# Indexer dots of two pieces in four banks, linear-attention outputs two chunks at a time, and a compression with operands swapped on column halves

## The reference, cut to what matters

```python
# front, NSA: 31 overlapping blocks of 32 tokens, 2 groups, keys and values
blk = kv[:, idx] + pe[None, None, :, None, :]
hid = silu(einsum('bnlgd,ldh->bngh', blk, w1))      # contraction over 32*64 = 2048, 128 hidden
kc_or_vc = einsum('bngh,hd->bngd', hid, w2)
nsa_gates = sigmoid(h @ w_in[:, 1792:1816])          # 24 columns
# layers, indexer: 8 heads of 64, for each block of 128 queries
dots = einsum('bqhd,bsd->bqhs', iqb, ik) * IDX_HD ** -0.5
score = einsum('bqhs,bqh->bqs', relu(dots), iwb)     # then the top 128 keys of each query
# layers, linear attention: 8 chunks of 64 tokens, 4 heads, keys of 64, values of 128
S_c = a * S_{c-1} + u_c
o = einsum('bnchk,nbhkv->bnchv', q, states)          # chunk c reads S_c
```

## Time and profile before

| | |
|---|---|
| median of 3 runs | 1949.58 us (1949.49 to 1950.72) |
| the profiled execution | 1950.57 us, its span 1948.8 us |
| PE busy | 1929.9 us (99%), 9837 matmul records |
| ACT, DVE, POOL busy | 894.7, 1159.9, 342.5 us (46%, 60%, 18%) |
| granted TensorE clock | 1.0 of full speed over the span |
| DMA | 178.87 MB, mean 92 GB/s |

### The profile page before, as it was taken

The page is one execution under the profiler, slowest core; times in us unless marked ns, Lnnn a source line. Parts: engine busy times, 40 slices in busy tenths (PEclk is TensorE's granted clock), DMA queues, the critical chain, the costliest instruction groups (busy, mean ns, idle before and its releaser), DMA issues.

```text
span 1948.8 us, 25508 instructions
## 1 busy us (share of the span) xinstructions
PE 1929.9 (99%) x9837; PEld 1559.7 (80%) x9837; DVE 1159.9 (60%) x1862; ACT 894.7 (46%) x1427; POOL 342.5 (18%) x172
## 2 busy tenths in 40 slices
PE   9999999999999999999999999999999999999999
PEld 7977777888888887788887787888788888788787
DVE  6867546585453557687555545466589545555443
ACT  5544455543333345533445454445443444545432
POOL 1010002211120122254010010232235110010211
PEclk9999999999999999999999999999999999999999
DMA  6211103223222333223122123224222212122321
GB/s 232 93 65 44 65 23 141 97 86 108 87 107 86 108 112 128 85 87 108 44 92 82 46 87 130 87 86 151 87 87 87 87 47 105 44 90 87 117 100 65
DMA packets 25735, 178.87 MB, mean 92 GB/s; under 512 B 2976, under 2 KB 3616, under 8 KB 5408
## 3 DMA queue, kind: packets, MB, share of 16 engines
q1 hardware_dynamic: 23904, 164.24, 23.4%
q10 hardware_dynamic: 1728, 13.24, 1.8%
HBM read 171.18 MB, written 6.29 MB: 91 GB/s over the span
## 4 chain that ended last, share of the span: by engine, by line
PE 94%; ACT 2%; DVE 2%; POOL 1%; DMA 1%; issue 0%; DVEq 0%; SPq 0%; ACTq 0%; POOLq 0%
PE pp L278 31%; PE pp L282 15%; PE pp L268 10%; PE pp L270 10%; PE pp L269 10%; PE po L278 3%; PE po L282 2%; PE po L805 1%; PE ps L1147 1%; PE ps L724 1%; PE pt L775 1%; PE ps L1098 1%; PE po L1082 1%; PE po L1034 1%; PE pt L1068 1%; DMA wraw<-weights 1%
## 5 line engine op out<-in xcount | busy, mean ns | idle before, releaser
L262 DVE TENSOR_TENSOR wlo<-wraw,whi 128x2048 fp32r<-128x2048 f32 x124 | 291.8, 2353 | 254.2 <-ACT whi L257 253.6
L257 ACT ACTIVATE whi<-wraw 128x2048 fp32r<-128x2048 f32 x150 | 286.3, 1909 | 48.5 <-PE pp L282 48.4
L278 PE MATMUL pp<-hhi,whi 128*128 128x512 f32 (+1 forms) x704 | 287.0, 408 | 1.0 <-DVE hlo L473 0.8
L278 PE MATMUL pp<-hlo,whi 128*128 128x512 f32 (+1 forms) x704 | 275.3, 391 | 0.0
L278 PE MATMUL pp<-whi,hhi 128*128 128x512 f32 x464 | 192.2, 414 | 0.0
L282 PE MATMUL pp<-hhi,wlo 128*128 128x512 f32 (+1 forms) x704 | 190.1, 390 | 0.0
L278 PE MATMUL pp<-whi,hlo 128*128 128x512 f32 x464 | 181.6, 391 | 0.0
L268 PE MATMUL pp<-split,whi 128*128 128x512 f32 x420 | 163.8, 390 | 0.0
L270 PE MATMUL pp<-split,wlo 128*128 128x512 f32 x420 | 163.4, 389 | 0.0
L269 PE MATMUL pp<-split,whi 128*128 128x512 f32 x420 | 163.4, 389 | 0.0
L1860 POOL TENSOR_TENSOR wlo<-wraw,whi 128x2048 fp32r<-128x2048 f32 x26 | 120.5, 4633 | 220.0 <-ACT whi L257 220.0
(11 more groups left out here) (419 smaller groups left out, 3476.9 us busy)
## 6 DMA issues: line engine op xcount, KB each, us to landing
wraw<-weights SPq DMA_DIRECT2D x150, 1024.0 KB, 4.8
out_t<-xT ACTq DMA_DIRECT2D x4, 1024.0 KB, 3.9
xT<-out_t ACTq DMA_DIRECT2D x2, 2048.0 KB, 8.7
wraw<-weights SPq DMA_DIRECT2D x4, 512.0 KB, 8.3
xT<-x_t SPq DMA_DIRECT2D x4, 512.0 KB, 8.8
work<-cmp_w ACTq DMA_DIRECT2D x1, 2048.0 KB, 7.5
xT<-x_t ACTq DMA_DIRECT2D x1, 2048.0 KB, 7.9
out_t<-xT SPq DMA_DIRECT2D x4, 512.0 KB, 2.6
```

Source lines behind the costliest of these rows:

```text
L257: nc.scalar.activation(whi[:, slot, :], wraw[:, slot, :], ACT.Copy).then_inc(w_hi, 1)
L262: nc.vector.tensor_tensor(wlo[:, slot, :], wraw[:, slot, :], whi[:, slot, :].bitcast(F32), ALU.subtract).then_inc(w_lo, 1)
L278: nc.tensor.matmul(out_ap, *pair, start=(start and n == 0 and part == 0), stop=False)
```

## The change

Four things, in the order of the diff: the indexer's dots of pieces p-1 and p are issued one behind the other after the `pe_wide` of the odd piece p, even pieces in `ps` and odd ones in `pt`; the turn of the head weights moves to p = 0 and to columns 480 to 511 of `pt[0]`, with a new wait `iw_kept` before the dots of piece 1. The outputs of chunks c-2 and c-1 are issued together at even c, ahead of `u`. The front's compression has the blocks stationary (62 columns) and w1 moving (128), keys on output partitions 0 to 61 and values on 64 to 125, alternating; its result is turned by two transposes between the tiles of `ksw`. The 24 gate columns are stored twice in the weight chunk, the second copy is overwritten by the low part (DVE works on 24 columns of each step in place of a whole chunk), and a step is one matmul with 48 and one with 24 stationary columns; the two sets of 24 rows are added where they are turned, by a float32 matmul with two stacked identities, and Sigmoid comes after it.

```diff
+        def dot_bank(p, g):
+            return (ps, pt)[p % 2][g]
         def pe_dots(pe, l, p):
...
-            if e >= 2:
-                pe.wait_ge(ix_relu, e)
+            if e >= 4:
+                pe.wait_ge(ix_relu, e - 2)
             for x, y in ((0, 0), (0, 1), (1, 0)):
                 for g in range(2):
-                    last = nc.tensor.matmul(ps[g][:, 0:w], iqr[x][rows, hp, i * P:i * P + P], ikr[y][rows, 0:w],
+                    last = nc.tensor.matmul(dot_bank(p, g)[:, 0:w], iqr[x][rows, hp, i * P:i * P + P], ikr[y][rows, 0:w],
...
@@ pe_layer, for p in range(12)
-                if p == 1:
+                if p == 0:
                     pe.wait_ge(evac, section("ikg", l)[2] + 1)
                     for i in range(QT):
-                        last = nc.tensor.matmul(pt[0][:, 8 * i:8 * i + 8], alr_f[64:72, i * P:i * P + P],
+                        last = nc.tensor.matmul(pt[0][:, 480 + 8 * i:488 + 8 * i], alr_f[64:72, i * P:i * P + P],
                                                 ident[64:72, 64:72], start=True, stop=True)
                     last.then_inc(iw_turned, 1)
-                pe_dots(pe, l, p)
+                if p % 2 == 1:
+                    pe_dots(pe, l, p - 1)
+                    if p == 1:
+                        pe.wait_ge(iw_kept, l + 1)
+                    pe_dots(pe, l, p)
...
@@ pe_layer, for c in range(8 + 1)
+                for past in (c - 2, c - 1) if c >= 2 and c % 2 == 0 else ():
+                    i = past // 2
+                    pe.wait_ge(state_ready, 8 * l + past + 1)
+                    if past >= 2:
+                        pe.wait_ge(go_out, 8 * l + past - 1)
+                    for hd in range(4):
...
+                    last.then_inc(gla_o, 1)
                 if c < 8:
...
-                        if c >= 2:
-                            pe.wait_ge(state_ready, 8 * l + c)
...
                     pe_wide(pe, "gz", l, c)
-                if c >= 1:
-                    i = (c - 1) // 2
...
@@ act_layer: the copies of outputs c-2 and c-1 at even c, and behind them act_wide of gz
...
@@ front, PE
+            pe.wait_ge(blk_ready, 2)
+            for x in range(16):
+                for kv in range(2):
+                    last = nc.tensor.matmul(ps[kv][hid_rows(kv), 0:P], blk_f[kv][:, x, :], w1_f[:, 16 * kv + x, :],
+                                            start=(x == 0), stop=(x == 15))
...
+            pe_tm_tile(pe, "ksw", None, 0)
+            pe_tm_tile(pe, "ksw", None, 1)
+            pe.wait_ge(hid_silu, 2)
             for kv in range(2):
-                pe.wait_ge(blk_ready, kv + 1)
-                for x in range(16):
-                    last = nc.tensor.matmul(ps[kv][:, 0:2 * N_CMP], w1_f[:, 16 * kv + x, :], blk_f[kv][:, x, :],
-                                            start=(x == 0), stop=(x == 15))
-                last.then_inc(hid_done, 1)
-            pe_tm(pe, "ksw", None, 256)
-            pe.wait_ge(hid_out, 1)
+                nc.tensor.transpose(pt[kv][:, 0:2 * N_CMP], hid_s[hid_rows(kv), :],
+                                    ident[hid_rows(kv), hid_rows(kv)]).then_inc(hid_turned, 1)
+            pe_tm_tile(pe, "ksw", None, 2)
+            pe_tm_tile(pe, "ksw", None, 3)
+            pe.wait_ge(hid_out, 2)
...
             def gates(bank):
                 for x in range(KT):
-                    last = three(bank[0:24, :], (wh[:, x, 0:24], wl[:, x, 0:24]), (hhi[:, x, :], hlo[:, x, :]),
-                                 x == 0, x == KT - 1)
-                return last
+                    if x < KT - 1:
+                        nc.tensor.matmul(bank[0:48, :], wh[:, x, 0:48], hhi[:, x, :], start=(x == 0), stop=False)
+                    last = nc.tensor.matmul(bank[0:24, :], wh[:, x, 0:24], hlo[:, x, :], start=False, stop=False)
+                return nc.tensor.matmul(bank[0:48, :], wh[:, KT - 1, 0:48], hhi[:, KT - 1, :], start=False, stop=True)
...
             for i in range(QT):
-                last = nc.tensor.transpose(po[0][:, 24 * i:24 * i + 24], g_fm[0:24, i * P:i * P + P],
-                                           ident[0:24, 0:24])
+                last = nc.tensor.matmul(po[0][:, 24 * i:24 * i + 24], g_fm[0:48, i * P:i * P + P],
+                                        cst[0:48, C_TWO:C_TWO + 24], start=True, stop=True)
@@ front, ACT: Silu on token rows, copies of the turned result after tile 1 of ksw
+            for kv in range(2):
+                act.wait_ge(hid_done, kv + 1)
+                nc.scalar.activation(hid_s[hid_rows(kv), :], ps[kv][hid_rows(kv), 0:P], ACT.Silu).then_inc(hid_silu, 1)
...
+            for n in range(QT):
+                act_tm_tile(act, "ksw", None, n, k_tm[:, n, :])
+                if n == 1:
+                    act.wait_ge(hid_turned, 1)
+                    nc.scalar.activation(hid_f[:, 0:2 * N_CMP], pt[0][:, 0:2 * N_CMP], ACT.Copy).then_inc(hid_out, 1)
...
@@ front, DVE, in place of dve_next(dve, "ksw", None)
+            nc.vector.tensor_tensor(low, wraw[:, slot, :].rearrange("p (k n) -> p k n", k=KT)[:, :, 24:48], low.bitcast(F32),
+                                    ALU.subtract).then_inc(w_lo, 1)
```

More of the change, by code:

```diff
@@ L72 @@
 C_E128 = 467
-NCST = 482
+C_TWO = 482
+NCST = 506
 M_ID, M_TRI, M_CH, M_CMP = 0, 128, 256, 384
@@ L604, in two_block_kernel @@
         blk_f = [wv(T + 4096 + 992 * kv, 16, 2 * N_CMP) for kv in range(2)]
-        hid_f = [wv(T + 6080 + 64 * kv, 64) for kv in range(2)]
+        hid_f, hid_s = wv(T + 6080, 64), wv(15168, P)
         cw2 = wv(T + 6208, 2, P)
@@ L1350, in pe_layer @@
             for c in range(8 + 1):
+                for past in (c - 2, c - 1) if c >= 2 and c % 2 == 0 else ():
[4 more added lines that the diff above has]
+                    for hd in range(4):
+                        rows, at = y_rows(hd % 2), P * (hd // 2)
+                        bank = D_BANKS[2 * (past % 2) + hd % 2]
+                        last = nc.tensor.matmul(bank[:, at:at + P], gq_f[rows, hd // 2, P * i:P * i + P],
+                                                st_f[past % 2][rows, hd // 2, :],
+                                                start=True, stop=True)
+                    last.then_inc(gla_o, 1)
                 if c < 8:
@@ L1559, in act_layer @@
                     act.dma_start(xT[:, :, :], out).then_inc(x_back, 16)
-                if c >= 1:
-                    i, rows = (c - 1) // 2, y_rows((c - 1) % 2)
-                    act.wait_ge(gla_o, 8 * l + c)
+                for past in (c - 2, c - 1) if c >= 2 and c % 2 == 0 else ():
+                    i, rows = past // 2, y_rows(past % 2)
+                    act.wait_ge(gla_o, 8 * l + past + 1)
                     for g in range(2):
-                        bank = D_BANKS[2 * ((c - 1) % 2) + g]
+                        bank = D_BANKS[2 * (past % 2) + g]
                         dst = a_f[rows, i, :].rearrange("p (h g d) -> p h g d", h=2, g=2)[:, :, g, :]
@@ L1567, in act_layer @@
                     last.then_inc(go_out, 1)
+                if half == 1:
+                    act_wide(act, "gz", l, t, z_a[:, t, :], ACT.Silu)
                 if c == 5:
@@ L2127, in _ @@
                                  bias=con(C_EPS)).then_inc(tm_root, 1)
-            act_tiles(act, "ksw", None, lambda bank, n, m: nc.scalar.activation(k_tm[:, m, :], bank[:, 0:256], ACT.Copy))
+            for n in range(QT):
[3 more added lines that the diff above has]
+                    nc.scalar.activation(hid_f[:, 0:2 * N_CMP], pt[0][:, 0:2 * N_CMP], ACT.Copy).then_inc(hid_out, 1)
+                    act.wait_ge(hid_turned, 2)
+                    for g in range(2):
+                        last = nc.scalar.activation(hidr[:, g, :, 0:N_CMP], pt[1][:, N_CMP * g:N_CMP * g + N_CMP].unsqueeze(1)
+                                                    .broadcast_to([P, 4, N_CMP]), ACT.Copy)
+                    last.then_inc(hid_out, 1)
             act.wait_ge(kvc_done, 1)
@@ L2459, in _ @@
             dve.drain().then_inc(tm_fin, 1)
-            dve_next(dve, "ksw", None)
+            c0, slot = section("ksw")[0] + 2, par_of("ksw", None)[1]
+            dve.wait_ge(w_hi, c0 + 1)
+            low = whi[:, slot, :].rearrange("p (k n) -> p k n", k=KT)[:, :, 24:48]
+            nc.vector.tensor_tensor(low, wraw[:, slot, :].rearrange("p (k n) -> p k n", k=KT)[:, :, 24:48], low.bitcast(F32),
+                                    ALU.subtract).then_inc(w_lo, 1)
             for x in range(2):
@@ L2700, in _stream @@
     put(kv[:, [3, 5]].reshape(D, 256))
-    put(np.pad(w[:, 1792:1816], ((0, 0), (0, 232))))
+    put(np.pad(np.tile(w[:, 1792:1816], 2), ((0, 0), (0, 208))))
     columns(w[:, 1816:3864])
@@ L2785, in _constants @@
     c[:, C_E128 + 7] = 1
+    c[0:48, C_TWO:C_TWO + 24] = np.tile(np.eye(24), (2, 1))
     c[:, C_S128], c[:, C_S64] = P ** -0.5, 64 ** -0.5
```

30 lines of the change are left out of this document (13 added, 17 removed).

## The result

The changed kernel takes 1937.98 us (median of 4 runs, 1936.84 to 1938.96); the kernel before, timed beside it, takes 1949.53 us. The ratio is 0.9939, with a 95% interval from 0.9922 to 0.9956: 11.6 us faster. The profiled execution took 1938.03 us, its span is 1936.2 us, the granted clock 1.0. The forecast was 1938.0 us.

A forecast was written before the change was run, and what follows sets the result against it. TensorE, busy 99% of the span, was taken as the bound. Layers 7.4 us plus front 4.3 us gave 11.7 us less than the profiled 1950.57 us, 1938.9, lowered to 1938.0 us for the runs' median; range 1936.0 to 1943.0 us.

The forecast's parts named there:

- indexer, per layer: Indexer dots in pairs: twelve excursions become seven, 2.4 us less per layer, bounds 1.15 and 2.8 us.
- compression: Front: 64 records on alternating column halves take 3.54 us in place of 7.09 us, 3.5 us less.
- turn of its result: Front: turning the compression's result adds an excursion and two records, 0.5 us more, bounds 0.3 and 0.8 us.
- turn of the gates: Behind the gates: four records become eight, 0.6 us more, bounds 0.2 and 0.7 us.
- The excursion: TensorE: leaving full-size matmuls for small products and returning costs 0.44 us, 0.21 to 0.22 us ahead and 0.23 us behind.
- The indexer's bound of 1.15 us: Indexer, per layer: dots gain nothing themselves; only five wide pieces gain, 5 x 0.23 us.
- The bound for halves that do not overlap: Compression: 0.144 us a record, 9.2 us in place of 3.5 us; as a rival 1943.7 us, chance 0.04.
- The favourable bound of 4.0 us: Compression: 4.0 us less in place of 3.5 us, if the fixed part is hidden.
- ksw: Front, tile 2 of these products: PE may wait a few tenths for ACT to evacuate tile 0; estimated gap 0.2 us.
- The gates' drain: Rival at the gates: 0.22 us at each of 15 column changes, 3.3 us back, 1941.3 us; chance 0.13.
- The top keys: DVE behind the indexer: slack before first scores falls from 3.1 to 1.4 us; rival of late keys 1942.8 us, chance 0.10.
- The slower rival: Two more POOL passes hit DVE's accumulations per layer, top keys end 7.7 us later, 1952.0 us; chance 0.03.

The follow-up runs named there:

- e1: The changed kernel with the indexer's dots issued piece by piece again, the turn of the head weights staying at p = 0: 1941.91 us, ratio to before 0.9965.
- e7: The changed kernel with the outputs of linear attention issued chunk by chunk again, as in the kernel before: 1940.23 us, ratio to before 0.9955.
- e5: The changed kernel with both compressions, keys and values, on output partitions 0 to 61, so on one column half: 1940.1 us, one profile.
- e9: The changed kernel with its front (compression, gates and their turn) as before, the layers staying changed: 1942.41 us, ratio to before 0.9966.
- e3: The changed kernel with dots over all 128 rows (two heads summed, another result) and issued piece by piece: 1946.73 us, one profile.
- e6: The changed kernel with 48 stationary columns in all sixteen gate matmuls, so none alternates (another result): 1937.7 us, one profile.
- e12: The changed kernel with six more unused MAX8 operations on VectorE at the end of the third row block's top keys: 1937.78 us, one profile.
- e4: The changed kernel with the three dots of one row half issued before those of the other, not alternating: 1937.0 us, one profile.

## Why the prediction was right

All numbers in us, for the whole kernel unless said.

| step | forecast | measured | by |
|---|---|---|---|
| indexer, per layer | -2.4 | -2.28, -2.32 | chain of waits; e1: 4.6 for two |
| linear attention, per layer | -1.3 | -1.29 | chain of waits; e7: 2.5 for two |
| compression | -3.5 | -3.45 | 7.09 to 3.64; e5: 7.13 |
| turn of its result | +0.5 | +0.51 | from the start of the compression to L1970 2.94 less, so 3.45 - 2.94; about 0.15 of it is an edge right behind the compression |
| gates | -1.85 | -1.81 | 3.86 against 5.67 |
| turn of the gates | +0.6 | +0.53 | from the start of L2015 to the wide piece: 5.35 against 4.82 |
| a wait of the front's scores | none | -0.5 | 1.2 to 0.7, unplanned |
| from the start, sum | -11.7 | -11.8 | e9: 7.0 layers, 4.8 front |

**The excursion.** The prediction read it as an edge of 0.21 us ahead and 0.23 us behind. That is right, and e3 shows what the rows before could not: for the dots it is the change of height. It is not the only change that does it, as the loads at the compression show. The indexer's bound of 1.15 us (edges that stay with the dots) is out.

**The compression** came 0.10 us above the estimate: a record costs 0.054 us rather than 0.0525 us, with the fixed part taken as 0.18 us. The bound for halves that do not overlap was taken from a row of 128 stationary columns, 0.144 us a record; e5 has 0.111 us. That rival would have come to 1941.5 us and not to 1943.7 us. The favourable bound of 4.0 us was a slip: with the fixed 0.18 us hidden it is 7.09 - 3.36 = 3.7 us. And the forecast gave the compression no edge on its far side; that edge, 0.32 against 0.18 us in the first matmul behind it, was covered only because the turn came out as much cheaper, about 0.36 us in place of 0.5 us.

**ksw.** The forecast saw a wait of a few tenths possible at tile 2. None came: the Silus are done at 75.4 us and tile 0 is evacuated at 77.45 us, before PE gets to tile 2 at 77.87 us.

**The gates' drain**, the likeliest rival, did not happen. The matmuls of 48 and of 24 columns follow each other every 0.23 us, and the load of 128 columns behind them starts as the last matmul of 48 columns does (102.55 us). The Trainium skill (TensorEngine Tiling (Array Packing), Key Properties) says that changing the mode drains TensorE. Where the height changes, the loads agree: 0.35 us idle at L1107, 0.36 us on the way back. Where only the number of columns changes, it depends: the float32 loads of the compression, 128 to 62 columns, agree (0.35 us), the fp32r gates do not, neither between 48 and 24 columns (3.86 us alternating, 3.87 us not, e6) nor from 48 to 128. There the measurement decides. That the type of the operands makes the difference is likely from these rows, but no run changed it alone.

**The top keys.** The step of the prediction that was furthest off: it left 1.4 us of the 3.1 us of slack, and 3.06 us are left. The direction of the cause was right. DVE's accumulations do end later against PE: they end 6.3 us earlier than before (815.61 against 821.92 us) where PE is there 7.66 us earlier, so DVE fell 1.4 us behind. (The estimate had been 2.4 - 0.8 = 1.6 us.) But I carried this delay on to the split as if DVE ran freely from there. It does not: two masking operations on the way stood stalled under a pass of POOL before (1.94 us for 256 columns at 841.60 us, 3.39 us for 512 at 906.04 us), and a late DVE merely stalls for less. The first of them already takes the whole 1.4 us back (0.58 us at 835.30 us). e12 shows the same for 4.6 us, with 3.0 us swallowed by the last. The slower rival was wrong for the same reason, on top of needing two passes that never came: the last stall alone would have swallowed some 3 of its 7.7 us.

**The medians** differ by 11.6 us, the stretches by 11.8 us. The forecast hit the median within 0.1 us, and that is luck: the layers gave 0.4 us less than forecast and the front 0.5 us more, by a wait that the forecast didn't have, and the start of the execution alone moves these profiles by up to 2.6 us.

## What to carry to other kernels

Count the changes of height in TensorE's sequence: each visit from 128-row to 64-row products and back costs 0.43 to 0.44 us here, for dots of 256 columns as for those of 512. Look at the loads too: a load that stands idle at a change marks an edge, also where only the width of float32 products changes. Group products of the same height with each other, if there are banks for their results; and keep the halves even so, since full height cost 7.5 us more than the visits. When a late engine runs into an operation that another engine stalls, its delay is absorbed up to the length of the stall, so a slack has to be followed to the end and not subtracted from. And take the wait at the start out of a comparison before counting tenths.

## What was not expected of the hardware

- The order in which the two row halves are issued makes no difference over three matmuls each: 0.69 us for six of 512 columns, alternating or one half after the other (e4).
- fp32r matmuls of 128 rows alternate between 24 and 48 stationary columns without a gap, at 0.232 us for 512 moving columns (e6), while the float32 loads of 62 columns behind 128 ones stand idle for 0.35 us.
- While POOL runs a pass of 4.6 us over 2048 columns, a masking operation of DVE on 512 columns grows from 0.43 to 3.38 us; MAX8 on the same operand does not grow (0.69 us each, four of the six wholly within the pass, e12).
- The last two of the eight records of the gates' turn (48 rows, matmuls at 107.36 and 107.47 us) run interleaved with the first of the 64-row score products behind them (107.25 and 107.42 us): these two do not wait for each other here.
